# RWKV gate in a two-block transformer kernel: both 128-row parts first, then the two 32-row parts in different row sets of the array

## The reference, cut to what matters

```python
D_GATE_LORA = max(32, int(round(0.6 * D_MODEL ** 0.8 / 32)) * 32)      # 160

def rwkv7_time_mix(h, ...):                                            # h: 256 x 1024
    ...
    g = jax.nn.sigmoid(xg @ g1) @ g2        # (256 x 160) @ (160 x 1024)
    ...
    y = wkv7(rh, wh, kh, vh, -kk, kk * ah)
    mean = jnp.mean(y, axis=-1, keepdims=True)
    var = jnp.mean(jnp.square(y - mean), axis=-1, keepdims=True)
    y = (y - mean) * lax.rsqrt(var + GN_EPS) * gn_g + gn_b
    y = y + jnp.sum(rh * kh * r_k, axis=-1, keepdims=True) * vh
    out = (y.reshape(B, T, C).astype(h.dtype) * g) @ wo
```

## Time and profile before

| | |
|---|---|
| time, median of 3 runs | 1394.63 us (1394.05 to 1394.86) |
| profiled execution, first to last instruction | 1392.2 us |
| what lies around the span (median less span) | 2.4 us |
| PE busy | 1362.8 us, 98% of the span |
| DVE / ACT / POOL busy | 855.2 / 696.6 / 38.1 us |
| mean granted TensorE clock | 1.000 |

### The profile page before, as it was taken

The page is one execution under the profiler, slowest core; times in us unless marked ns, Lnnn a source line. Parts: engine busy times, 40 slices in busy tenths (PEclk is TensorE's granted clock), DMA queues, the critical chain, the costliest instruction groups (busy, mean ns, idle before and its releaser), DMA issues.

```text
span 1392.2 us, 23783 instructions
## 1 busy us (share of the span) xinstructions
PE 1362.8 (98%) x8927; PEld 1117.8 (80%) x8927; DVE 855.2 (61%) x1234; ACT 696.6 (50%) x1110; POOL 38.1 (3%) x42
## 2 busy tenths in 40 slices
PE   8999999999999999999999999999999999999998
PEld 7888877778888878888787688778888887788887
DVE  4545577875755464445784788766555677555554
ACT  5444456675465464444554444235444566644442
POOL 0000000000000000000001000110000010000000
PEclk9999999999999999999999999999999999999999
DMA  8655545556444565555352101314555651265552
GB/s 294 214 181 181 181 140 202 167 188 200 161 163 157 148 207 197 189 195 186 115 196 77 61 4 33 112 46 166 181 189 184 227 175 52 83 212 194 182 184 104
DMA packets 145537, 220.25 MB, mean 158 GB/s; under 512 B 16761, under 2 KB 65295, under 8 KB 145329
## 3 DMA queue, kind: packets, MB, share of 16 engines
q1 hardware_dynamic: 145456, 219.14, 47.8%
HBM read 218.04 MB, written 1.05 MB: 157 GB/s over the span
## 4 chain that ended last, share of the span: by engine, by line
PE 88%; DVE 6%; ACT 3%; issue 1%; POOL 1%; DMA 1%; SPq 0%; DVEq 0%; ACTq 0%; POOLq 0%
PE acc L291 12%; PE acc L293 12%; PE gp L291 12%; PE acc L292 12%; PE gp L293 12%; PE gp L292 12%; PE tp L944 1%; PE gp L2767 1%; PE acc L2782 1%; DVE sb_w_lo L280 1%; PE acc L1280 1%; PE tp L291 1%; ACT sb_w_hi L264 1%; ACT sb_arena L407 1%; DMA sb_raw<-in_ffn_w 1%
## 5 line engine op out<-in xcount | busy, mean ns | idle before, releaser
L280 DVE TENSOR_TENSOR sb_w_lo<-sb_raw,sb_w_hi 128x1024 fp32r<-128x1024 f32 (+1 forms) x380 | 451.5, 1214 | 207.4 <-ACT sb_w_hi L264 205.7
L264 ACT ACTIVATE sb_w_hi<-sb_raw 128x1024 fp32r<-128x1024 f32 (+1 forms) x380 | 387.9, 1052 | 210.9 <-PE acc L293 106.9
L291 PE MATMUL gp<-sb_w_hi,sb_xa_hi 128*128 128x512 f32 (+1 forms) x752 | 298.5, 397 | 5.0 <-DVE sb_w_lo L280 3.5
L293 PE MATMUL gp<-sb_w_lo,sb_xa_hi 128*128 128x512 f32 (+1 forms) x752 | 291.7, 388 | 0.0
L292 PE MATMUL gp<-sb_w_hi,sb_xa_lo 128*128 128x512 f32 (+1 forms) x752 | 291.2, 387 | 0.0
L291 PEld LDWEIGHTS gp<-sb_w_hi,sb_xa_hi 128*128 128x128 f32 x752 | 141.3, 188 | 37.8 <-DVE sb_w_lo L280 6.7
L293 PEld LDWEIGHTS gp<-sb_w_lo,sb_xa_hi 128*128 128x128 f32 x752 | 141.2, 188 | 29.6
L292 PEld LDWEIGHTS gp<-sb_w_hi,sb_xa_lo 128*128 128x128 f32 x752 | 141.5, 188 | 27.1 <-issue 0.5
L291 PE MATMUL acc<-sb_w_hi,sb_mid_hi 128*128 128x512 f32 x400 | 156.2, 390 | 0.0
L293 PE MATMUL acc<-sb_w_lo,sb_mid_hi 128*128 128x512 f32 x400 | 155.8, 390 | 0.0
L292 PE MATMUL acc<-sb_w_hi,sb_mid_lo 128*128 128x512 f32 x400 | 155.7, 389 | 0.0
(11 more groups left out here) (417 smaller groups left out, 1756.8 us busy)
## 6 DMA issues: line engine op xcount, KB each, us to landing
sb_raw<-in_ffn_w SPq DMA_DIRECT2D x264, 256.0 KB, 4.3
sb_raw<-in_mlp_w SPq DMA_DIRECT2D x256, 256.0 KB, 2.9
sb_raw<-in_w_in SPq DMA_DIRECT2D x72, 256.0 KB, 3.2
sb_raw<-in_a_w_rkv SPq DMA_DIRECT2D x48, 256.0 KB, 4.1
sb_raw<-in_xattn_w_kv SPq DMA_DIRECT2D x32, 256.0 KB, 3.6
sb_raw<-in_w_out SPq DMA_DIRECT2D x16, 256.0 KB, 3.2
sb_raw<-in_xattn_w_q SPq DMA_DIRECT2D x16, 256.0 KB, 3.1
sb_raw<-in_xattn_w_o SPq DMA_DIRECT2D x16, 256.0 KB, 3.1
```

The costliest lines, as they stand in the source:

```text
L264: A.e.activation(w_hi[:, s, :, 0:n], raw[:, r, :, 0:n], ACT.Copy).then_inc(hi_done, 1)
L280: V.e.tensor_tensor(w_lo[:, s, :, 0:n], raw[:, r, :, 0:n], w_hi[:, s, :, 0:n].bitcast(F32), ALU.subtract).then_inc(lo_done, 1)
L291: e.matmul(dst, xh, wh, start=start, stop=False)
L293: return e.matmul(dst, xh, wl, start=False, stop=stop)
```

## The change

The gate of a token half is now made in another order and with other rows: `pe_gate_high` for b = 0 and b = 1 (128 rows each), then `pe_gate_low`, which issues both 32-row parts one behind the other. The one for b = 0 stands in rows 0 to 31 of the array and writes to `gp`, the one for b = 1 in rows 32 to 63 and writes to `tp`. For that the sigmoid of the last 32 gate rows is written twice by ACT, to partitions 32 to 63 and to 0 to 31, and the last 32 rows of `g2` are loaded in two DMAs of 32x512 in place of one of 32x1024. The semaphore target for the loads grows from 64 to 80. In token half 0 all four gate matmuls stand ahead of `pe_xy(last, 3)`, where two of them stood behind it.

```diff
@@ sp
-                sp.dma_start(flat(1, 1024, 1024)[0:32, :], a["a_g2_2"][0][128:160, :]).then_inc(self.g2_loaded, 16)
+                for b, at in enumerate(self.GATE_ROWS):
+                    sp.dma_start(self.g2_low(b), a["a_g2_2"][0][128:160, b * 512:(b + 1) * 512]).then_inc(self.g2_loaded, 16)
@@ act_rows
-                A.e.activation(self.sig_g[0:32, 1, :], tp[0:32, 1, 256:512], ACT.Sigmoid).then_inc(*A.one(self.low))
+                A.e.activation(self.sig_g[self.GATE_ROWS[1], 1, :], tp[0:32, 1, 256:512], ACT.Sigmoid).then_inc(*A.one())
+                A.e.activation(self.sig_g[self.GATE_ROWS[0], 1, :], tp[0:32, 1, 256:512], ACT.Sigmoid).then_inc(*A.one(self.low))
@@
-            def pe_gate(self, T, t, b):
-
-                dst = self.spare_bank(b)
-                T.e.matmul(dst, self.sig_g[:, 0, t * P:(t + 1) * P], flat(1, b * 512, 512), start=True, stop=False)
-                T.e.matmul(dst, self.sig_g[0:32, 1, t * P:(t + 1) * P], flat(1, 1024 + b * 512, 512)[0:32, :], start=False,
-                           stop=True).then_inc(*T.one(self.gate))
+            GATE_ROWS = (slice(0, 32), slice(32, 64))
+
+            def g2_low(self, b):
+                return flat(1, 1024 + b * 512, 512)[self.GATE_ROWS[b], :]
+
+            def pe_gate_high(self, T, t, b):
+
+                T.e.matmul(self.spare_bank(b), self.sig_g[:, 0, t * P:(t + 1) * P], flat(1, b * 512, 512), start=True, stop=False)
+
+            def pe_gate_low(self, T, t):
+
+                for b, at in enumerate(self.GATE_ROWS):
+                    T.e.matmul(self.spare_bank(b), self.sig_g[at, 1, t * P:(t + 1) * P], self.g2_low(b), start=False,
+                               stop=True).then_inc(*T.one(self.gate))
@@ pe_core
-                T.e.wait_ge(self.g2_loaded, 64)
+                T.e.wait_ge(self.g2_loaded, 80)
                 T.e.wait_ge(self.y_done, last)
-                self.pe_gate(T, 0, 0)
+                self.pe_gate_high(T, 0, 0)
+                self.pe_gate_high(T, 0, 1)
+                self.pe_gate_low(T, 0)
                 self.pe_xy(T, last, 3)
-                self.pe_gate(T, 0, 1)
@@ pe_out
                 for b in range(2):
-                    self.pe_gate(T, 1, b)
+                    self.pe_gate_high(T, 1, b)
+                self.pe_gate_low(T, 1)
```

## The result

| | before | after |
|---|---|---|
| time, median (20 runs each) | 1394.61 us (1393.79 to 1397.09) | 1397.55 us (1395.62 to 1403.15) |
| ratio, 95% interval | | 1.0028 [1.0021, 1.0036] |
| profiled execution, first to last instruction | 1392.2 us | 1399.7 us (its time: 1401.65 us) |
| mean granted clock of that execution | 1.000 | 0.995 |

The kernel became slower by 0.28%, clear of the noise by its interval. The forecast of 1395.9 us was too low, and the median lies above the range.

A forecast was written before the change was run, and what follows sets the result against it. Although PE is 98% busy, DVE's chain was taken to bound the gates, so PE's saving gains nothing. +0.43 (token half 0) and +0.86 (token half 1) make +1.29 us on 1394.63: 1395.9 us, range 1394.3 to 1397.2.

The forecast's parts named there:

- What bounds the kernel: Around the gates: DVE's chain releases PE's next work, so PE's saving of 1.24 us per token half gains nothing.
- The pair runs beside each other: The two 32-row gate matmuls on PE share their time entirely, 0.86 us together.
- one after the other: Rival: the 32-row parts take 1.72 us in sequence; +2.15 us in all, 1396.8 us; chance 0.19.
- the next load 0.9 us on: Sign in the profile after: the load following the two 32-row loads comes 0.9 us behind them.
- the sum of 2.96 us: PE's gate time per token half: 0.19 + 1.72 + 0.19 + 0.86 us, against 4.20 before.
- Token half 0, +0.43: Ahead of the output product: `pe_xy(last, 3)` loads 0.86 us later, so DVE's mean comes 0.43 us later.
- token half 1, +0.86: Output stage: DVE's gate 0 waits for a matmul now third instead of second, shifting everything behind it by 0.86 us.
- The new wait ahead of `pe_z(last, 4)`: Token half 0: PE's `pe_z(last, 4)` stands behind `dve_x` for some 0.5 us, without delaying the output product.
- The second sigmoid hidden: ACT's extra 32x256 sigmoid, at most 0.37 us, is covered by a 1.54 us wait ahead of 734.44.
- The gaps are hardly longer than known ones: PE's standstills of about 2.0 and 2.3 us, against 1.6 and 1.5 known: argument against a fall of the clock.
- The rival had the place and the size off: Clock rival: longer standstills bring 1.2 GHz, work behind 922 runs at half speed, +10 us, 1406 us; chance 0.04.
- One more DMA issue on SP … 0.43 us: SP's extra `g2` load delays the queued weight loads 0.43 us, covered since they are used after 922.

The follow-up runs named there:

- h2: h1 with both 32-row parts in rows 0 to 31, one sigmoid and 4 idle matmuls in the second fill; 1395.80 us, ratio 1.0012.
- h1: f1 with SP's weight loads behind `g2` held back to about 902 us; 1394.27 us, ratio 0.9997.
- e8: Kernel before plus one 0.69 us VectorE instruction between token half 0's second gate and the mean; 1400.84 us, ratio 1.0044.
- e1: Kernel after with 14 idle matmuls in each of PE's two standstills, ahead of the output product and of the second transposes; 1397.61 us, ratio 1.0022.
- f2: Kernel after with SP's weight loads behind `g2` held back until token half 0's second gate is done; 1395.83 us, ratio 1.0016.
- f3: Kernel before with SP's weight loads behind `g2` held back some 20 us; 1393.30 us, ratio 0.9989.
- k1: Kernel before with only the load of `g2`'s last 32 rows split into two DMAs of 32x512; 1395.16 us, ratio 1.0004.
- e3: Kernel after with 14 idle matmuls only in the second standstill, ahead of the second transposes; 1402.32 us, ratio 1.0045.
- f1: Kernel after with 7 idle matmuls in each of PE's two standstills; 1396.47 us, ratio 1.0017.
- g1: Kernel after with `pe_xy(last, 3)` ahead of the pair, one token-half-1 gate in the first standstill, an output chunk between the transposes; 1392.92 us, ratio 0.9988.
- e2: Kernel after with 14 idle matmuls only in the first standstill, ahead of the output product; 1397.14 us, ratio 1.0024.

## Why the prediction was wrong, and where it was right

**What bounds the kernel: right.** The gates lie on DVE's chain, and PE's saving is worth nothing. PE's work fell by 1.24 us per token half as worked out (2.97 us measured for the gate, 2.96 forecast), and both standstills grew instead. The Trainium skill (TensorEngine Tiling (Array Packing), "PSUM Bottleneck"), which the prediction cited, says that tiling speeds up TensorE and not the emptying of PSUM, which may become the bound. The trace agrees in part: the chain that bounds here begins with such a reading of PSUM (`dve_gate`) and goes on with other work of DVE, and PE's waits for it grew from 1.5 to 2.13 us and from 0.3 to over 2 us.

**The pair runs beside each other: right.** Starts 0.01 us apart, 0.85 us saved against h2. The rival "one after the other" is out; h2 is that case, and it loses 0.85 us more in token half 0, where 0.86 was forecast. (The sign "the next load 0.9 us on" left out the change of shape that the sum of 2.96 us has; it is 1.06.)

**Token half 0, +0.43, and token half 1, +0.86: right.** The trace has 0.43 and, at the second transposes, 0.85; h1 has 0.43 and 0.87 in the same places without a fall of the clock. The runs of after at clock 1.000 are 1.0 to 1.35 us above before, where the sum had 1.29. That these runs hit the sum is in part luck: they also hold the longer issue wait, which the sum lacked, and they have 0.2 us less around the span, which it did not foresee. The new wait ahead of `pe_z(last, 4)`, "some 0.5 us", is 0.53.

**The second sigmoid hidden: right.** ACT's timeline, against the earlier trace rows:

```profile
732.04 0.37 ACT L2666 ACTIVATE sb_arena<-tp 32x256 f32<-32x256 f32 x1 [1.90 <-PE tp L2473]
732.44 0.37 ACT L2667 ACTIVATE sb_arena<-tp 32x256 f32<-32x256 f32 x1
733.95 1.02 ACT L2670 ACTIVATE sb_arena<-acc 128x1024 f32<-128x1024 f32 x1 [1.14 <-PE acc L2504]
```

The second one took 0.40 us out of a wait of 1.54.

**"The gaps are hardly longer than known ones", chance 0.04: the step that failed.** The prediction named the mechanism, forecast both gaps (2.0 and 2.3 us, measured 2.13 and 2.20), and saw that waits of 1.5 and 1.6 us had left the clock alone. From that it concluded that 2.1 us would too. Nothing in the trace supported that: its waits end at 1.6 us, so it said nothing of longer ones. e8 shows that the same growth by itself, with no change to the gate, puts most runs at clock 0.994 to 0.997. e1 shows that without the gaps no run falls. The rival had the place and the size off. It let the clock fall only behind 922 us, where the longer stretch came behind the first gap, at 907.6. And it took all of the output product to run at half speed, +10 us; the clock came back, and the two stretches cost 4.5 and 1.5 us in the profiled run, less or nothing in others. The median pays some 1.6 us for it (2.9 less 1.3), if the whole difference between the median and the runs at 1.000 is put down to the clock.

**"One more DMA issue on SP … 0.43 us": a wrong cover, a smaller error.** I asked when the moved transfers are needed (late enough) and didn't ask what else uses the DMA engines. The issues, against the earlier trace rows:

```profile
881.01 0.90 SPq L2270 DMA_DIRECT2D sb_arena<-in_a_g  x2
```

Instructions come over the same DMA engines, and PE's issue wait was 0.55 us longer. That the burst causes this wait is shown (f2, f3: it disappears with the burst, and 1.1 us of time with it in f3). That what PE waits for is the block of instructions is read from the constant 1.3 to 1.5 us between the two, and that the split load is what lengthens it is only supported (k1).

**What stays open.** Whether the clock falls in a given run, and how often, has no explanation here. Nor has the time around the span: it is 2.1 to 2.2 us in every run of f3 and of before (where the span is on record), but 1.9 to 2.0 in every run of after, f2 and h1, so that 0.2 us of what the traces show does not reach the times. It has to be set apart before the sums are compared. The spans of after at clock 1.000 are 1393.7 to 1394.0 us, 1.5 to 1.8 above the 1392.2 of the profile of before; 1.29 from the chain and 0.55 from the issue wait make 1.84. h1 against f3, where the issue wait is gone, is +1.0 us in time and +1.1 in the median span, against 1.3 by the aligned traces.

## What to carry to other kernels

When a saving falls on an engine that is then released by another engine's chain, the saving becomes a longer standstill, and on TensorE that can cost more than nothing: read off how long the wait will be, and if it becomes longer than any in the trace, don't take a fall of the clock as remote. First move work that is ready into the hole, then shorten PE's work; the change that cost 2.9 us with its first schedule holds a pair that is worth some 0.6 to 0.9 us in a filled one. Bulk loads that are not needed yet are not free where they are issued, since instructions arrive over the same DMA engines.

## What the runs showed of the hardware

- Standstills of PE of 1.5 and 1.6 us (before) left the granted clock at 1.00. With one of 2.1 us (after, e3, e8, f2) 19 of 44 runs had a mean clock of 0.994 to 0.996, and none of 219 other runs had. In the profiles the clock fell within 1.2 us of the end of standstills of 2.13 and 2.20 us (after), 2.12 us (e3) and 1.67 us (f1, g1), and stayed at 1.00 behind 2.11 us (e8), 2.18 us (e2), and 2.12 and 2.20 us (f2). The stretches at 0.50 lasted 3.4, 6.8, 10.2 and 13.7 us.
- Float32 matmuls of 32 rows in rows 0 to 31 and 32 to 63, with different banks, run beside each other: 0.87 us for two of 512 columns (after), 1.72 in the same rows (h2). The change of shape behind them costs a further 0.19 us.
- PE stopped for 0.57 to 1.67 us, until 1.3 to 1.5 us behind the end of a block of instructions, while loads at up to 404 GB/s filled the DMA engines (ten kernels); with those loads held back it stopped for 0.09 us (f3).
